# One short matmul in front of each column group of the up products

## The reference, cut to what matters

```
gu = h @ w_ffn_in[l]                      # first block: 2048 -> 2 x 5632
g_ffn, u_ffn = jnp.split(gu, 2, axis=-1)
y = (jax.nn.silu(g_ffn) * u_ffn) @ w_ffn_out[l]
...
u = causal_depthwise_conv(h @ w_ffn_up[i], w_ffn_conv[i], b_ffn_conv[i])   # second block
u_gate, u_val = jnp.split(u, 2, axis=-1)
x = x + (jax.nn.gelu(u_gate) * u_val) @ w_ffn_down[i]
```

## Time and profile before

| | us |
|---|---|
| median of 3 runs | 2819.76 (2814.05 to 2823.84) |
| the profiled execution's own time | 2819.68 |
| its span, first to last instruction | 2818.0 |
| TensorE busy | 2718.0 (96% of the span) |
| VectorE busy | 1809.7 (64%) |
| ScalarE busy | 1295.5 (46%) |

### The profile page before, as it was taken

One profiled execution on the slowest core, in us unless ns is written; L12 is line 12 of the kernel. 1 busy time (PEld: TensorE's weight loads), 2 busy tenths in 40 slices (PEclk: granted clock), 3 DMA queues, 4 the chain that ended last, 5 costly groups with the idle time before them and its releaser, 6 DMA issues.

```text
span 2818.0 us, 38907 instructions
## 1 busy us (share of the span) xinstructions
PE 2718.0 (96%) x14799; PEld 2338.9 (83%) x14799; DVE 1809.7 (64%) x2009; ACT 1295.5 (46%) x1556; POOL 291.9 (10%) x161
## 2 busy tenths in 40 slices
PE   4899999999989999999997999999999999999998
PEld 4798888788788888888886989878888888888887
DVE  7976779689965556555566444656666654666655
ACT  2356554334444444444444444635555533555454
POOL 2010121100001100001000000100113110131100
PEclk8899999999999999999998999999999999999999
DMA  9975646598945557755567554445555565555553
GB/s 373 347 267 192 217 146 224 191 342 294 337 135 193 184 204 254 244 188 180 192 238 243 167 165 151 152 153 176 183 190 194 179 199 188 189 183 186 187 196 133
DMA packets 299522, 588.70 MB, mean 209 GB/s; under 512 B 12282, under 2 KB 19438, under 8 KB 298510
## 3 DMA queue, kind: packets, MB, share of 16 engines
q1 hardware_dynamic: 292816, 577.84, 60.2%
q10 hardware_dynamic: 6590, 9.27, 1.0%
HBM read 584.98 MB, written 2.10 MB: 208 GB/s over the span
## 4 chain that ended last, share of the span: by engine, by line
PE 89%; DVE 6%; issue 2%; ACT 1%; DMA 1%; POOL 0%; SPq 0%; DVEq 0%; POOLq 0%; ACTq 0%; PEldq 0%
PE psum L782 13%; PE psum L786 13%; PE psum L784 13%; PE bank L975 12%; PE psum L975 11%; PE bank L978 6%; PE psum L978 6%; PE psum L793 2%; PE psum L797 2%; PE psum L795 2%; DVE ada_acc L866 2%; PE bank L948 1%; DVE w_lo L740 1%; DVE mod_acc L651 1%; PE bank L2596 1%
## 5 line engine op out<-in xcount | busy, mean ns | idle before, releaser
L740 DVE TENSOR_TENSOR w_lo<-raw,w_hi 128x1024 fp32r<-128x1024 f32 x912 | 1161.1, 1290 | 831.0 <-ACT w_hi L728 821.0
L728 ACT ACTIVATE w_hi<-raw 128x1024 fp32r<-128x1024 f32 x912 | 953.2, 1054 | 1271.2 <-PE psum L786 575.9
L975 PE MATMUL psum<-h_both,w_hi 128*128 128x512 f32 x1408 | 494.8, 395 | 0.7 <-DVE x L2364 0.7
L975 PE MATMUL bank<-h_both,w_hi 128*128 128x512 f32 x1408 | 493.4, 394 | 0.0
L978 PE MATMUL bank<-h_both,w_lo 128*128 128x256 f32 x1408 | 394.8, 280 | 0.0
L978 PE MATMUL psum<-h_both,w_lo 128*128 128x256 f32 x1408 | 394.7, 280 | 0.0
L782 PE MATMUL psum<-w_hi,h_both 128*128 128x512 f32 x880 | 346.5, 394 | 4.1 <-DVE w_lo L740 1.5
L786 PE MATMUL psum<-w_hi,h_both 128*128 128x512 f32 x880 | 342.8, 389 | 0.0
L784 PE MATMUL psum<-w_lo,h_both 128*128 128x512 f32 x880 | 342.6, 389 | 0.0
L975 PEld LDWEIGHTS psum<-h_both,w_hi 128*128 128x128 f32 x1408 | 263.9, 187 | 62.3 <-DVE x L2364 1.1
L975 PEld LDWEIGHTS bank<-h_both,w_hi 128*128 128x128 f32 x1408 | 263.9, 187 | 61.5
(11 more groups left out here) (361 smaller groups left out, 3173.4 us busy)
## 6 DMA issues: line engine op xcount, KB each, us to landing
raw<-in_w_in_dram SPq DMA_DIRECT2D x120, 1024.0 KB, 5.1
raw<-in_w_ffn_in_dram SPq DMA_DIRECT2D x88, 1024.0 KB, 5.0
raw<-in_w_ffn_up_dram SPq DMA_DIRECT2D x88, 1024.0 KB, 5.1
raw<-in_w_ada_dram SPq DMA_DIRECT2D x64, 1024.0 KB, 5.1
raw<-in_w_ffn_out_dram SPq DMA_DIRECT2D x44, 1024.0 KB, 5.2
raw<-in_w_ffn_down_dram SPq DMA_DIRECT2D x44, 1024.0 KB, 5.1
ada_raw<-in_w_ada_dram SPq DMA_DIRECT2D x64, 512.0 KB, 8.4
raw<-in_w_out_dram SPq DMA_DIRECT2D x32, 1024.0 KB, 5.2
```

The costliest lines, as they stand in the source:

```text
L728: nc.scalar.activation(w_hi[:, slot, :, 0:ncol], raw[:, rs, 2 * h:2 * h + 2, 0:ncol], ACT.Copy).then_inc(split_hi, inc)
L740: nc.vector.tensor_tensor(w_lo[:, slot, :, 0:ncol], raw[:, rs, 2 * h:2 * h + 2, 0:ncol], w_hi[:, slot, :, 0:ncol].bitcast(F32), ALU.subtra ...
L975: pe.matmul(region[:, f, :].rearrange("p (s t) -> p s t", s=2), w_hi[:, slot, kk, cols_], h_both[:, :, k, :], start=first, stop=False, ski ...
```

## The change

In `half`, the inner function of `up_products`, one matmul is put in front of the loop over the tiles, for the first row tile of a group and only where the loop begins with tile 0. It multiplies the stationary tile that the group's first product also uses with the first 128 columns of `h_hi`, and writes them to the first 128 columns of the region's first bank. The first product, which starts a new sum (`start=first`), overwrites them. No semaphore is touched.

```diff
@@ -970,6 +970,9 @@
                     k = ph.halves[idx][3] + kk
                     first = idx == start and kk == 0
                     last = idx == stop - 1 and kk == 1
+                    if first and fs[0] == 0:
+                        pe.matmul(region[:, 0, 0:P], w_hi[:, slot, 0, 0:P], h_hi[:, k, 0:P], start=True, stop=True,
+                                  skip_group_check=True)
                     for f in fs:
                         cols_ = slice(f * P, (f + 1) * P)
                         pe.matmul(region[:, f, :].rearrange("p (s t) -> p s t", s=2),
```

## The result

The changed kernel takes 2832.28 us in the median of 6 runs (2831.06 to 2833.02), the kernel before 2819.39 us in 6 runs beside them: a ratio of 1.0045, with a 95% interval of 1.0035 to 1.0055, 12.9 us slower. The profiled execution took 2832.29 us, 12.6 more than that of before. One run of the kernel before, of the 21 beside e5 to e8, took 6427.66 us and is left out of every comparison. The likeliest time of the forecast was 2824.4, with a range of its own of 2821 to 2828, which the measured time is outside of. The full range, 2813 to 2834, holds it, because the rival that was priced at 2833.6 is in the main what happened.

What follows compares the result with a forecast made beforehand. TensorE, busy without a gap in the up products, was taken to bound the kernel. 43 extra matmuls at 0.110 us, 4.7 us, on 2819.68 gave 2824.4 us, own range 2821 to 2828, full range 2813 to 2834.

Steps and rivals of the forecast that it cites:

- the rival that was priced at 2833.6: First parts' 22 groups thrown onto the longer step: 22 x 0.42 = 9.2 us on top, 0.5% slower; chance 0.14.
- What bounds the kernel: Up products: TensorE busy without a gap, weights ready ahead, so whatever lengthens TensorE's stream lengthens the kernel.
- The count and the price: Up products: 44 matmuls and 44 weight loads added, 43 of them counting at 0.110 us each, 4.7 us.
- the load of its own full tile: New matmul: loading its 128 x 128 stationary tile, not its moving columns, most likely sets the step of about 0.110 us.
- The bounds of 0.06 and 0.23: New matmul's price: from half a 256-column step to a 512-column step, 2.6 to 9.9 us for 43.
- steps unchanged or mixed both ways: Likeliest case, up products: matmul costs 0.06 to 0.12 us, pair steps unchanged or mixed, 2824.4 us; chance 0.50.
- the longer step in the first parts: Rival: first parts' 22 groups go from 0.347 to 0.353 us a pair, 9.2 us more, 2833.6; chance 0.14.
- the ten runs of pairs behind L948's matmuls: Behind L948's 128-column matmuls, eight runs of pairs had the shorter step, two the longer; used against the longer-step rival.
- the prediction's own sign: Prediction is wrong if group distances change by other than one short matmul's price, or stretches outside the up products change.
- The rival of the shorter step everywhere: Second parts' 20 groups go onto the shorter step, 20 x 0.42 = 8.4 us back, 2816.0 us; chance 0.18.
- The price of 512 columns: Rival: new matmul costs as much as one of 512 columns, 43 x 0.23 = 9.9 us, 2829.6; chance 0.12.
- the matmul for nothing: Rival: the matmul fits where TensorE waits in the up products, time stays at 2819.7 us; chance 0.06.

Runs made afterwards that it cites:

- e5: Kernel before, no extra matmul; g = 0 groups do tiles 0, 1 for three halves, taking out the up products' one wait: 2818.83 us, ratio 1.0005.
- e8: Changed kernel with two extra matmuls of 32 stationary columns, instead of one of 128, in front of all 44 groups: 2834.95 us in one run.
- e1: Changed kernel with the extra matmul only in front of the 20 groups of the second parts: 2820.41 us, ratio 1.0009 to the kernel before.
- e3: Changed kernel with all 44 extra matmuls at 32 stationary columns instead of 128: 2833.75 us in one run.
- e2: Changed kernel with only two extra matmuls, in front of the second group of each FFN's first part: 2827.67 us, ratio 1.0036.
- e6: Against e5: two 128-column matmuls at each second part's first group, first iteration outside TensorE's loop: 2810.65 us, ratio 0.9975 to the kernel before.
- e7: Changed kernel with two extra matmuls of 128 columns, instead of one, in front of all 44 groups: 2838.01 us in one run.
- e4: Kernel before, second parts' first iteration out of TensorE's loop, first group behind one 256-column matmul (first FFN) or two of 128 (second): 2816.22 us.

## Why the forecast's likeliest case was wrong and its range right

**What bounds the kernel**: right. TensorE has no gap in the up products after the change either, and no wait was added.

**The count and the price**: right in size. 44 matmuls and 44 loads were added. The price was put at 0.110 us and is 0.11 (22.72 - 22.61, e1). Of the two reasons beside it, the load of its own full tile was wrong: e3 left the price as it was. The other, that the following product's load has only 128 columns to hide behind, is what e3 and e8 show. The bounds of 0.06 and 0.23 held. The Trainium skill's 81 ns (TensorE: Matmul & The Clock Gate, Back-to-back issue gap), weighed in the prediction, is below every price measured here with a full tile behind.

**The step that failed** in the likeliest case is the forecast's "steps unchanged or mixed both ways" at 0.50, against 0.14 for "the longer step in the first parts". It weighed the ten runs of pairs behind L948's matmuls as if they told what the new matmul would do: "matmuls of this size led to the shorter step eight times in ten". They have another predecessor, and eight of them in a row. With one float32r matmul of 128 columns in a stream on the shorter step, the first group behind went to the longer step in e2 in both FFNs. In the changed kernel and e1 it is the same each time that a group finds the stream on the shorter step, 8 of 8. It was 19 of 22 groups, so 2833.6 was nearly the result: 22 x 0.42 was 9.2 us, measured were 8.0. By the prediction's own sign, group distances that change by other amounts than one short matmul's price, its first case was wrong. The full range held because this rival was priced, at a chance of 0.14; that the time came within 1.3 us of the rival's is in part luck, since three groups stayed shorter, some second-part groups became shorter, and the stretches outside added to it.

**The rival of the shorter step everywhere** (0.18) had the mechanism right and the matmul wrong: one in front of each group does not do it, two at the entry of a second part do (e6). In e7, with two in front of every group, the first group of the first FFN's second part took 22.41 us, the shorter step, and the next was on the longer one again.

**A row that was read too far**: both second parts at the longer step were taken as one rule, the step of a stream behind 512-column products. In the second FFN it was a draw: e2's profile has it at the shorter step from the wait of the earlier trace rows on, and without the wait the lower cluster of runs is gone (e5). The forecast called 9.8 us between three runs a spread without asking what lay behind it; some 4 us of it can be this draw. A smaller one: that float32r takes a step by its columns from 256 up is shown by the starts of the earlier trace rows (0.12) and the earlier trace rows (0.23), not by the overlapping durations of the earlier trace rows.

**The price of 512 columns and the matmul for nothing**: both fell, with 0.11 us for one matmul in front of a full tile in every run.

## What to carry to other kernels

Where one engine is busy without a gap, compare the distance of equal pieces of work at different places before pricing an edit: two steps for the same instructions mean that an edit may move the stream from one to the other, and that can be worth more than the edit itself. Such a change is found by group distances in the timeline. Waits and the chain looked the same on both sides here, and TensorE's busy time showed that 12.3 us were added, but not where or why. Take runs that fall into two clusters as a question, and look for a wait that ends at a time of its own.

## What the runs showed of the hardware that was not expected

A stream of pairs of 512 and 256 moving columns has two steady paces at one granted clock of 1.00, 0.347 and 0.353 us a pair, 22.19 and 22.61 us for 64 pairs. It holds either one over 10 groups, 220 us and more, until something of another length stands in it, or a wait. Which it takes follows in part from what stands in front: one matmul of 128 columns in a stream on the shorter pace led to the longer one (ten times in ten: six in the changed kernel, two in e1, two in e2). On the longer pace the same matmul mostly changed nothing, but led to the shorter in 4 of 34 groups of the changed kernel, so it is not a rule by the pace alone. Behind 512-column products the pace was the longer one, also with one matmul of 128 (e1) or 256 columns (e4) in between, and the shorter with two of 128 (e6, both FFNs). Behind the wait it was one or the other with the same instructions (the kernel before and e2). Why there are two paces was not tried, and stays open.
